# adaLN panel groups moved out of the first feed-forward into later stages of a decoder layer

## What is computed

```
mod = silu(c) @ w_ada + b_ada                       # 9 vectors of 2048 per condition
sh1, sc1, gt1, shm, scm, gtm, sh2, sc2, gt2 = split(mod, 9)
h = h + 0.5 * gt1 * swiglu(modulate(h, norm1, sh1, sc1), w_up1, w_down1)
xm = modulate(h, norm_mix, shm, scm)
proj = xm @ w_in                                    # q/k/v of both mixers, z, gates
oA = gated_deltanet(proj);  oB = dilated_window_attention(proj)
h = h + gtm * ((sig(gA) * (oA @ w_proj_a) + sig(gB) * (oB @ w_proj_b)) @ w_out)
h = h + 0.5 * gt2 * swiglu(modulate(h, norm2, sh2, sc2), w_up2, w_down2)
y = rmsnorm(h)
```

## Time and profile before

| | us |
|---|---|
| median of 3 runs | 2980.79 (2974.71 to 2981.76) |
| the profiled execution, its own time | 2972.28 |
| its span, first to last instruction | 2970.5 |
| mean granted TensorE clock | 0.963 of full speed |

### The profile page before, as it was taken

The page is one execution under the profiler, slowest core; times in us unless marked ns, Lnnn a source line. Parts: engine busy times, 40 slices in busy tenths (PEclk is TensorE's granted clock), DMA queues, the critical chain, the costliest instruction groups (busy, mean ns, idle before and its releaser), DMA issues.

```text
span 2970.5 us, 52363 instructions
## 1 busy us (share of the span) xinstructions
PE 2777.4 (94%) x21861; PEld 2582.1 (87%) x21861; DVE 1378.2 (46%) x1714; ACT 1063.8 (36%) x1080; POOL 12.5 (0%) x32
## 2 busy tenths in 40 slices
PE   5799999999999989899999699987999999999998
PEld 2588889988889978799996599977989999999998
DVE  0433345443334565545555455535454445444444
ACT  1334333333333332443331244423344433333332
POOL 0000000000000000000000000000000000000000
PEclk8899999999999989999998799999999999999999
DMA  9768775677774567623332444474435545545443
GB/s 388 299 269 298 276 269 167 217 293 282 283 286 164 187 245 267 248 105 122 128 114 93 179 159 167 152 262 173 168 142 184 173 146 180 198 180 184 155 157 128
DMA packets 91639, 600.53 MB, mean 202 GB/s; under 512 B 10112, under 2 KB 10240, under 8 KB 32656
## 3 DMA queue, kind: packets, MB, share of 16 engines
q1 hardware_dynamic: 89296, 586.26, 54.4%
q0 software_dynamic: 1808, 11.55, 1.0%
q10 hardware_dynamic: 432, 1.21, 0.1%
HBM read 586.36 MB, written 12.62 MB: 202 GB/s over the span
## 4 chain that ended last, share of the span: by engine, by line
PE 81%; DMA 10%; ACT 4%; DVE 4%; issue 2%; ACTq 0%; SPq 0%; DVEq 0%
PE acc L1623 22%; PE acc L1624 21%; PE acc L1631 20%; DMA raw<-in_up 5%; ACT whi L660 3%; PE mp L1681 2%; PE acc L1834 2%; PE acc L1829 2%; PE acc L1828 2%; DMA raw<-in_ada 2%; DMA raw<-in_win 2%; DVE wlo L1036 1%; PE mp L1691 1%; PE mp L1708 1%; PE mp L1900 1%
## 5 line engine op out<-in xcount | busy, mean ns | idle before, releaser
L1036 DVE TENSOR_TENSOR wlo<-raw,whi 128x2048 fp32r<-128x2048 f32 (+2 forms) x445 | 929.8, 2090 | 991.7 <-ACT whi L660 991.4
L660 ACT ACTIVATE whi<-raw 128x2048 fp32r<-128x2048 f32 (+2 forms) x445 | 779.3, 1751 | 1126.1 <-PE acc L1631 718.4
L1623 PE MATMUL acc<-xhi,whi 128*128 128x264 f32 x4048 | 1030.4, 291 | 51.4 <-ACT whi L660 51.4
L1624 PE MATMUL acc<-xlo,whi 128*128 128x264 f32 x4048 | 1015.8, 288 | 0.0
L1623 PEld LDWEIGHTS acc<-xhi,whi 128*128 128x128 f32 x4048 | 775.2, 192 | 106.5 <-issue 58.1
L1624 PEld LDWEIGHTS acc<-xlo,whi 128*128 128x128 f32 x4048 | 776.5, 192 | 0.6
L1631 PE MATMUL acc<-xhi,wlo 128*128 128x264 f32 x4048 | 529.9, 284 | 0.0
L1631 PEld LDWEIGHTS acc<-xhi,wlo 128*128 128x128 f32 x4048 | 504.5, 188 | 0.0
L1623 PE MATMUL acc<-uhi,whi 128*128 128x264 f32 x1408 | 360.8, 292 | 17.1 <-DVE ulo L1171 17.1
L1624 PE MATMUL acc<-ulo,whi 128*128 128x264 f32 x1408 | 354.0, 287 | 0.0
L1623 PEld LDWEIGHTS acc<-uhi,whi 128*128 128x128 f32 x1408 | 270.2, 192 | 18.7 <-DVE ulo L1171 17.7
(11 more groups left out here) (323 smaller groups left out, 1868.3 us busy)
## 6 DMA issues: line engine op xcount, KB each, us to landing
raw<-in_up SPq DMA_DIRECT2D x176, 1024.0 KB, 4.9
raw<-in_ada SPq DMA_DIRECT2D x144, 1024.0 KB, 6.5
raw<-in_down SPq DMA_DIRECT2D x128, 704.0 KB, 4.1
raw<-in_win SPq DMA_DIRECT2D x69, 1024.0 KB, 5.1
raw<-in_wgate SPq DMA_DIRECT2D x32, 1024.0 KB, 4.9
raw<-in_wout SPq DMA_DIRECT2D x16, 1024.0 KB, 4.9
raw<-in_wproj SPq DMA_DIRECT2D x24, 512.0 KB, 4.4
raw<-in_cache SPq DMA_DIRECT2D x12, 1024.0 KB, 6.4
```

The costliest lines, as they stand in the source:

```text
L660: act.activation(whi[:, s.slot(SPLIT), 0:width], raw[:, r.slot(RAW), 0:width], ACT.Copy)\
L1036: v.tensor_tensor(wlo[:, s.slot(SPLIT), 0:width], raw[:, r.slot(RAW), 0:width], whi[:, s.slot(SPLIT), 0:width].bitcast(F32), ALU.subtract)\
L1623: mm(dst, w, xh, start=starts and k == 0, stop=False)
L1624: mm(dst, w, xl, start=False, stop=False)
```

## The change

The groups are spread otherwise: 8 at the start as before, 12 in the first feed-forward (6 in each half), 6 in QKV as before, 2 in the B projections, 4 in the output stage, 4 in the first half of the second feed-forward. The sum is again 36, and each vector is still done before its use.

Two orders of a body exist now. `MIXED` is the old one. `WIDE` has eight weight panels and four adaLN panels, none of them side by side. A half of the first feed-forward is five wide bodies and one mixed; the first half of the second one is four wide bodies and three bodies of four plain panels (`PLAIN`). In the B projections each round's 512 KB load is followed by one adaLN panel's, and TensorE does `ada` behind each round's matmuls; the fold of the first group is behind the fifth round, that of the second behind the first two output panels. The output stage is four mixed bodies. `stretches` gives, for each body of a plan, its number of rounds and where its panels, slots and groups begin; `spot` says in which slot a panel lies. Because `csl` and `arow` have to stay until the second feed-forward, some buffers of the mixers get other places in SBUF (`bD`, `bA`, `qs`, `snq`, `sqk`, `svn` over the area of the small norm buffers; `ks`, `awide`, `mgd`, `sqo` behind `arow`). Each stage waits for the number of groups that it needs (`G_QKV`, `G_FF2`, ...) in place of the old counts.

```diff
-ADA_HALF = 4 * UP_IT
-ADA_MIX = ADA_FIRST + 2 * ADA_HALF
-G_FIRST, G_MIX, G_ALL = ADA_FIRST // 4, ADA_MIX // 4, NADA // 4
+PLAIN = (0, 1, 2, 3)
+MIXED = (0, 1, None, None, 2, None, None, 3)
+WIDE = (0, 1, None, 2, 3, None, 4, 5, None, 6, None, 7)
+FF1_PLAN = ((WIDE, 5), (MIXED, 1))
+FF2_PLANS = ((WIDE, 4), (PLAIN, 3)), ((PLAIN, UP_IT),)
+G_FF1_HALF = 6
+G_FIRST, G_ALL = ADA_FIRST // 4, NADA // 4
+G_QKV = G_FIRST + 2 * G_FF1_HALF
+G_PB = G_QKV + CT // 4
+G_OUT = G_PB + 2
+G_FF2 = G_OUT + KD // 4
...
-BODY = (0, 1, None, None, 2, None, None, 3)
-AHEAD = (4, 7, 8, 9)
...
-R3 = R2 + N_CACHE
+R_PB = S_PB + R2 + N_CACHE
+R_OUT = R_PB + KD
+R_FF2 = R_OUT + 2 * KD
...
+def spot(body, x):
+
+    n = count(body)
+    return body.index(x) if x < n else len(body) + x - n
...
+def stretches(plan):
+
+    p = r = g = 0
+    for body, rounds in plan:
+        yield body, rounds, p, r, g
+        p, r, g = p + rounds * count(body), r + rounds * len(body), g + rounds * (None in body)
...
+def r_pb(k):
+
+    return At(R_PB + 2 * k if k < KD // 2 else R_OUT + k - KD // 2)
...
+            def body_loads(body, r0, w, w0, g0, i):
+
+                n, m = count(body), 0
+                for k, x in enumerate(body):
                     if x is None:
-                        load(seq(r0 + k, 8, i), t["ada"][i * 4 + (a0 + n)])
-                        n += 1
+                        load(seq(r0 + k, len(body), i), t["ada"][i * 4 + (4 * g0 + m)])
+                        m += 1
                     else:
-                        load(seq(r0 + k, 8, i), w[i * 4 + (w0 + x)])
-
-            def ffn(r0, up, down, o, ada):
-                with sp.Fori(0, UP_IT) as i:
-                    if ada:
-                        mixed_body(r0, up, UP * o, ADA_FIRST + o * ADA_HALF, i)
-                    else:
-                        for k in range(4):
-                            load(seq(r0 + k, 4, i), up[i * 4 + (UP * o + k)])
-                rd = r0 + (8 if ada else 4) * UP_IT
+                        load(seq(r0 + k, len(body), i), w[i * n + (w0 + x)])
...
+            def ffn(r0, up, down, o, plan, g0):
+                for body, rounds, p, r, g in stretches(plan):
+                    with sp.Fori(0, rounds) as i:
+                        body_loads(body, r0 + r, up, UP * o + p, g0 + g, i)
...
             for k in range(KD // 2):
-                r = At(R3 + S_PB + k)
+                r = r_pb(k)
                 sp.wait_ge(slot_done[r.slot(RAW)], r.turn(RAW).val())
                 sp.dma_start(raw[:, r.slot(RAW), 0:W_B].rearrange("p (k c) -> p k c", k=2),
                              t["wproj"][2 * k:2 * k + 2, :, W_A:PROJ * P].rearrange("k p c -> p k c"))\
                   .then_inc(panel_loaded[r.slot(RAW)], 16)
+                load(r + 1, t["ada"][4 * G_PB + k])
             with sp.Fori(0, KD // 4) as i:
-                for k in range(4):
-                    load(seq(R3 + S_OUT + k, 4, i), t["wout"][i * 4 + k])
+                body_loads(MIXED, R_OUT, t["wout"], 0, G_OUT, i)
             for o in range(2):
-                ffn(R3 + S_FF2 + o * FF_HALF, t["up2"], t["down2"], o, False)
+                ffn(R_FF2 + o * (FF_HALF + 4 * (G_ALL - G_FF2)), t["up2"], t["down2"], o, FF2_PLANS[o], G_FF2)
...
+            def ffn(n, o, s0, r0, a0, plan, g0, last):
+                for body, rounds, p, r, g in stretches(plan):
+                    per, raws = count(body), len(body)
+                    with act.Fori(0, rounds) as i:
+                        for u in range(per // 2):
+                            s = seq(s0 + p + 2 * u, per, i)
+                            a = seq(a0 + p + 2 * u, per, i)
+                            done(s)
+                            act.activation(sg[:, u % 2, :], acc[:, a.slot(BANKS), 0:NT], ACT.Silu)\
+                               .then_inc(acc_taken[a.slot(BANKS)], 1)
+                            split_hi(s + 2, seq(r0 + r + spot(body, 2 * u + 2), raws, i))
+                            if None in body and u == per // 2 - 1:
+                                copy_rows(seq(g0 + g, 1, i), seq(r0 + r + last_ada(body), raws, i))
+                            split_hi(s + 3, seq(r0 + r + spot(body, 2 * u + 3), raws, i))
+
+                            wait_taken(act, a + 1)
+                            act.activation(uhi[:, tiles(p // 2 + u, i, per // 2), :], hf[:, u % 2:u % 2 + 1, :], ACT.Copy)\
+                               .then_inc(hidden_hi, 1)
+                sd = s0 + UP
+                shift = r0 + sum(len(body) * rounds for body, rounds in plan) - sd
...
                 done(At(S_PB + k))
-                split_hi(At(S_PB + k + 2), R3, W_B if k + 2 < KD // 2 else PANEL)
+                split_hi(At(S_PB + k + 2), r_pb(k + 2), W_B if k + 2 < KD // 2 else PANEL)
+                if k % 4 == 3:
+                    copy_rows(At(G_PB + k // 4), r_pb(k) + 1)
                 act.wait_ge(merged_ready, k + 1)
                 act.activation(xhi[:, 2 * k:2 * k + 2, :], mgd[:, 2:4, :], ACT.Copy).then_inc(merged_hi, 1)
             ready_root()
             with act.Fori(0, KD // 4) as i:
                 for k in range(4):
-                    split_hi(seq(S_OUT + 2 + k, 4, i), R3)
+                    if k == 3:
+                        copy_rows(seq(G_OUT, 1, i), seq(R_OUT + last_ada(MIXED), 8, i))
+                    split_hi(seq(S_OUT + 2 + k, 4, i), seq(R_OUT + spot(MIXED, k + 2), 8, i))
                     tile_square(sqo, N_SQ, T_OUT, k, i)
...
+                if k == 5:
+                    take_ada(G_PB, 0)
+            set_gate(GTM, 1.0, G_QKV + KD // 4)
             dve.wait_ge(h_loaded, 16)
+            take_ada(G_PB + 1, 0)
             with dve.Fori(0, KD // 4) as i:
                 for k in range(4):
                     take_sublayer(seq(S_OUT + k, 4, i), seq(A_OUT + k, 4, i), k, i, 4, T_OUT)
-                    split_lo(seq(S_OUT + 2 + k, 4, i), R3)
+                    split_lo(seq(S_OUT + 2 + k, 4, i), seq(R_OUT + spot(MIXED, k + 2), 8, i))
+                take_ada(G_OUT, i)
             own_taken(A_FF2 - 1)
             dve.wait_ge(h_tile, T_OUT + KD)
...
+            def panels(body, s0, r0, a0, g0, i, ready=None, made=x_lo, behind=None):
+
+                p, n = 0, count(body)
                 g = seq(g0, 1, i)
+                for k, x in enumerate(body):
                     if ready and x == 0:
+                        duo(At(s0), At(r0), At(a0), made, ready)
                     elif x is None:
+                        ada(p, g, seq(r0 + k, len(body), i))
                         p += 1
+                    elif not (ready and x == 1):
+                        full(seq(s0 + x, n, i), seq(r0 + k, len(body), i), seq(a0 + x, n, i), xs)
+                    if behind and x is not None:
+                        behind(x, i)
+                if p:
+                    fold(g)
+
...
+            def ffn(n, o, s0, r0, a0, plan, g0, ready=None):
+                for body, rounds, p, r, g in stretches(plan):
+                    first = 0
+                    if ready and p == 0:
+                        panels(body, s0, r0, a0, g0, 0, ready)
+                        first = 1
+                    with pe.Fori(first, rounds) as i:
+                        panels(body, s0 + p, r0 + r, a0 + p, g0 + g, i)
...
-                panel(At(S_PB + k), R3, [(to(a), bs, True, True), (to(a + 1), bs, True, True)])
-
-            def out_body(i):
-                for k in range(4):
-                    full(seq(S_OUT + k, 4, i), R3, seq(A_OUT + k, 4, i), xs)
-                    tile_sum(sqo, N_SQ, k - 1, i)
-
-            duo(At(S_OUT), At(R3 + S_OUT), At(A_OUT), merged_lo, lambda k: k // 2 + 1)
-            tile_sum(sqo, N_SQ, 0, 0, first=True)
-            full(At(S_OUT + 2), R3, At(A_OUT + 2), xs)
-            tile_sum(sqo, N_SQ, 1, 0)
-            full(At(S_OUT + 3), R3, At(A_OUT + 3), xs)
...
+            def out_sums(x, i):
+                if isinstance(i, int) and x == 0:
+                    fold(At(G_PB + 1))
+                else:
+                    tile_sum(sqo, N_SQ, x - 1, i, first=isinstance(i, int) and x == 1)
+
+            panels(MIXED, S_OUT, R_OUT, A_OUT, G_OUT, 0, lambda k: k // 2 + 1, merged_lo, out_sums)
             with pe.Fori(1, KD // 4) as i:
-                out_body(i)
+                panels(MIXED, S_OUT, R_OUT, A_OUT, G_OUT, i, behind=out_sums)
             tile_sum(sqo, N_SQ, 3, 3, last=True)
             for o in range(2):
-                ffn(1, o, S_FF2 + o * FF_HALF, R3 + S_FF2 + o * FF_HALF, A_FF2 + o * A_FF_HALF, False,
-                    None if o else lambda k: N_FIRST + KD + 1 + k + 2)
+                ffn(1, o, S_FF2 + o * FF_HALF, R_FF2 + o * (FF_HALF + 4 * (G_ALL - G_FF2)), A_FF2 + o * A_FF_HALF,
+                    FF2_PLANS[o], G_FF2, None if o else lambda k: N_FIRST + KD + 1 + k + 2)
 
```

More of the change, by code:

```diff
@@ L171, with count, last_ada @@
 W_Z, W_BA, W_DWA = CT, CT + H, CT + H + 1
+def count(body):
+    return sum(x is not None for x in body)
+def spot(body, x):
```

(33 more changed lines are left out.)

145 lines of the change are left out of this document (45 added, 100 removed).

## The result

| | before | after |
|---|---|---|
| median of 8 runs each, us | 2977.09 (2972.50 to 2981.76) | 2984.52 (2980.48 to 2989.57) |
| the profiled execution's own time | 2972.28 | 2983.18 |
| its span | 2970.5 | 2981.2 |
| mean granted TensorE clock | 0.963 | 0.959 |

The ratio is 1.0024, with a 95% interval from 1.0013 to 1.0036: slower by 7 us, where the forecast had 18.9 us less. It lies inside the 0.3% that the prediction called no change in practice, and outside its range.

What follows compares the result with a forecast made beforehand. TensorE, busy 94% of the span, was taken as the bound, so only its waits could be won. Terms -69.6 + 20.8 + 21.9 + 8 = -18.9 us, taken from the median 2980.8, gave 2962; range 2945 to 2976.

Steps and rivals of the forecast that it cites:

- part 3: Output stage: four old-style bodies add 5.5 us each, the sum of squares standing inside the late load's time: +21.9 us.
- Part 1: First feed-forward: five wide bodies of 52.0 us without waits and one old-style body per half; in all -69.6 us.
- the 2.8 us of the first two bodies: First feed-forward: later landings make the first two bodies 2.8 us longer than steady ones; the wide ring covers them: -2.8.
- Part 2: Second feed-forward, first half: four wide bodies each add 5.2 us, with no wait to fill: +20.8 us.
- Part 4: B projections: two groups in eight rounds, with rounds, entry, exit and reload of h: +8 us, bounds 0 and 15.
- Entry: Start of the B projections: the second projection panel waits for a cache panel's slot; up to +3.0, taken as 1.6 us.
- The reload: B projections: POOL reads back 2,112 KB of h while little DMA rate is spare: +2.6 us.
- The rounds: B projections: the alternating ring makes rounds 4.6 us instead of 4.26: +2.8 us for eight.
- The exit: End of the B projections: the second output panel waits for the slot of the seventh adaLN panel: +1 us.
- C: First and second feed-forward: each of 14 wide bodies keeps a 0.97 us wait; change -5.3, time 2975.5 us; chance 0.16.
- D: B projections: ring closes over two rounds, not three, costing 37 us instead of 8; time 2991 us; chance 0.09.
- the forecast's own chain: B projections: landing, splits, product, TensorE work and handovers take the landing plus 7.4 us for three rounds.

Runs made afterwards that it cites:

- the late reload: Changed kernel, but POOL reads h back after the eighth round of the B projections, not the fourth: 2978.05 us, 1.0011 of the kernel before.
- three edits: Changed kernel with output squares before splits, h read back after the eighth round, and adaLN panels ahead of waiting first tiles: 2954.61 us, 0.9928 of the kernel before.
- the kernel that leaves the third edit out of the output stage: Kernel with three edits, but the third edit kept only in the up stages and QKV: 2956.06 us, 0.9931 of the kernel before.
- the third edit: adaLN panels before tile 2 multiplied ahead of a stage's two waiting first tiles; alone on the kernel before: 2966.61 us, 0.9966.

## Why the prediction was wrong

**The step that failed** is one sentence of part 3: "A panel with its sum of squares is now 6.30 us, so the 0.45 of the sum stands inside the time that the late load has." It took the sum as work on TensorE, free to lie in the landing. It is a wait as well: the sum needs ScalarE's square, ScalarE serves its splits and squares in program order, and the split in front of it is that of the very panel that lands late. The rows for it were there, since the kernel before has the same order; but without adaLN panels the output loads land early (4.9 us in the median, and ScalarE waits for none of them in the stage), and the order costs nothing. With nothing but this order changed the kernel takes 2967.47 us, inside the prediction's range.

The arithmetic of the loss, from the rows after: TensorE's waits for squares 15.2 us against 3.8; four pairs 3.54 + 3.57 + 2.95 + 3.57 = 13.6 instead of 7.6; and three sums of 1.25 instead of 0.45, 2.4 more. That is 11.4 + 6.0 + 2.4 = 19.8, less the four times 0.52 that part 3 had for the wait, 17.7, beside the 19.4 by which the stage missed its term. Not all of it is the order's: with the square first, 3.3 us of waits for squares and a slow first pair (3.58 us, in the first body) are still there. What went is 11.9 of waits, 4.4 of the other three pairs and 2.4 of the sums, 18.7; what came is 2.4 of waits for the late split itself (1.75, 0.34 and 0.32). That makes 16.3, beside the 16.4 measured. The difference repeats: three executions with the square first and no other edit of this stage take 132.0, 132.2 and 133.4, three without it 147.2, 148.4 and 148.9. What is left of the stage, 132.0 - 107.1 = 24.9, is 3 over part 3's 21.9 and 1.1 over its upper bound; the slow first pair is 1.7 of it, and why it is slow stays open.

**Part 1 right in mechanism, mis-sized by 6.2.** The wait in each body went away. A wide body after is 52.35 us, not 52.0, with nothing between its matmuls:

```profile
221.04:273.39 52.35, 52.35 (x426) 48.42 (x426) 21.53 (x17) 19.45 (x18) 0.00 (x0) 1.00 0.62 240
```

Inside it the starts of the closing matmuls around one adaLN panel are 7.02 to 7.03 apart and plain ones 5.84 to 5.85 (226.72, 233.75 and 239.59), so a panel alone costs 1.17 and not 1.08: going over and back costs 0.21, not 0.12. The Trainium skill, TensorEngine Tiling (Array Packing), Key Properties, has that drain but no time for it; the trace agrees in kind. This is 10 x 0.35 = 3.5 of the miss. The mixed body that ends each half has the landing of its last panel at 7.91 us instead of 6.5, with 10.1 instead of 8.86 between the closing matmuls, another 1.2; in the second half that landing is 6.40 and costs nothing. The remaining 1.5 or so is in the first half too, where part 1 had taken back the 2.8 us of the first two bodies. But from its first up matmul to its first down matmul this half takes from 298.7 to 301.7 us in the five executions with the same code, so the remainder is no more than their spread.

**Part 2 right:** +20.0 for 20.8.

**Part 4 right in kind, 5 short.** Entry, given 1.6, cost nothing that shows: the stretch up to the B projections got no longer. The reload was given 2.6 and takes 6.4, because its 2,112 KB go beside the panel on which the next round waits. The rounds were given 2.8: the middle ones are 5.0 to 6.0 where 4.6 was taken, and with the late reload the eighth round still starts 35.2 us behind the first instead of 29.5, so 5.8. The projection panels' landings have a median of 7.9 us in this window where its 4.6 us rounds went by 5.5 to 6.6, and the fold behind the fifth round, 0.99 us, had no term at all. The exit, given 1.0, is 1.1. The rule of the Trainium skill that the prediction set aside (DMA: Bandwidth & Descriptors, Where 436 GB/s comes from) would have given an estimated +12 for part 4, near the 12.9 (13.3 - 0.4). The trace doesn't bear out its reason: in the 13.3 us in which that panel was under way the 16 DMA engines moved

```profile
1965.82:1979.08 13.26, 8.74 (x70) 6.67 (x69) 4.38 (x9) 2.35 (x3) 0.56 (x1) 0.95 0.96 386
```

386 GB/s at 0.96 of their time, above the 358 of the Trainium skill's page, which is one core's half of what a stack of HBM gives to two; here one core works.

**The rivals.** C, a wait kept in each wide body, did not come. Of D there is one long round, 13.07 us behind the longest landing, and with it one of the prediction's signs of being wrong, a round over 6. But it doesn't need D's mechanism: the forecast's own chain, the landing and 7.4 us for three rounds, gives 13.3 + 7.4 = 20.7 for it, and the last three rounds took 5.00 + 5.33 + 13.07 = 23.4, the eighth of them at a granted clock of 0.56 (1982.18 to 1988.70). And to turn the sign D needed a part 4 of 27 us; it came to 12.9. None of the rivals was a stall in the output stage. The prediction looked for a load that is late, and did not ask which instructions of other engines stand behind the wait for it.

## What to carry to other kernels

Before work is put into a stage to fill a landing, read the programs of the other engines there for what stands behind the wait for that load. An order that is harmless while loads land early becomes the bound as soon as one is late, and then the work put there as a filler is locked out of the gap that it should fill. Operations that wait for nothing late (here the square, and the copy of the rows) go ahead of the one that waits for a DMA. And a bulk transfer with no hurry should not be issued beside a panel that is next in a chain.

## What the runs showed of the hardware

An adaLN pair of sixteen 128x32 matmuls takes 1.92 us at full clock, and 3.57 to 3.64 after TensorE has idled for 4.46 us (with a sum of squares between) or 7.63 us; two matmuls of a sum of squares go from 0.45 to 1.25. So the stall of 4.46 us cost about 2.5 more in what followed it, an estimate from these rows (1.7 and 0.8). Shorter stalls don't decide it: behind idle times of 1.99, 2.81 and 2.31 us, each with a sum of squares between, a pair took 3.54 and 2.95 us in the changed kernel and 3.58 in that with three edits, and behind the same 2.31 us it took 1.92 in the kernel that leaves the third edit out of the output stage. What decides there stays open.

A load of 512 KB was split 13.3 us after its issue when a 2,112 KB read of another queue was issued 0.7 us after it, and 6.7 us after its issue where that read came later.
